# Four conv inputs per layer transposed by VectorE and DRAM scratch instead of TensorE

## The reference, cut to what matters

```python
CONV_WIDTH = 4

def causal_depthwise_conv(x, w, b):
    y = lax.conv_general_dilated(
        x, w[:, None, :], window_strides=(1,), padding=[(CONV_WIDTH - 1, 0)],
        dimension_numbers=('NWC', 'WIO', 'NWC'), feature_group_count=x.shape[-1])
    return y + b

    (aq, ak, av, ag, su, sv, sg, mq, mk, mv, mo, mg, mi, mf) = split_columns(x @ w_in)
...
    qk = jax.nn.silu(causal_depthwise_conv(jnp.concatenate([mq, mk], axis=-1), conv_w, conv_b))
    mq, mk = jnp.split(qk, 2, axis=-1)
...
    h = mlstm_chunkwise(heads(mq), heads(mk) * (MLSTM_HEAD_DIM ** -0.5), heads(mv), ig, lf)
```

## Time and profile before

| what | us |
|---|---|
| median of three runs | 1271.83 (1271.44 to 1271.86) |
| span of the profiled execution, first to last instruction | 1269.9 |
| its own time | not given apart from the three runs; 1.9 lies between its span and their median |
| TensorE busy | 1257.0 (99% of the span) |
| VectorE busy | 893.0 (70%) |
| ScalarE busy | 705.4 (56%) |
| GpSimd busy | 244.0 (19%) |
| DMA, mean | 209 GB/s |

### The profile page before, as it was taken

How to read it: one execution, slowest core, us unless ns; L and a number is a source line. 1 busy time by engine, 2 the same in 40 slices (tenths; PEclk the granted TensorE clock), 3 DMA queues, 4 the chain that set the end, 5 groups by cost and what they waited for, 6 DMA issues and landing times.

```text
span 1269.9 us, 16388 instructions
## 1 busy us (share of the span) xinstructions
PE 1257.0 (99%) x6342; PEld 1040.2 (82%) x6342; DVE 893.0 (70%) x1229; ACT 705.4 (56%) x989; POOL 244.0 (19%) x268
## 2 busy tenths in 40 slices
PE   9999999999999999999999999999999999999996
PEld 8888888878888888888888788888888888888885
DVE  5686876876667655865785779768665776567656
ACT  5477476575555544444563775666755555345441
POOL 0321522522220000400003223334131200004000
PEclk9999999999999999999999999999999999999998
DMA  9968768765665555465657587678546556565562
GB/s 336 310 209 261 236 189 277 260 192 164 204 195 174 184 186 185 152 230 190 207 186 238 183 282 245 193 258 282 184 149 215 183 157 209 165 197 198 186 212 86
DMA packets 129277, 264.97 MB, mean 209 GB/s; under 512 B 8824, under 2 KB 8976, under 8 KB 128688
## 3 DMA queue, kind: packets, MB, share of 16 engines
q1 hardware_dynamic: 123712, 247.23, 60.6%
q0 software_dynamic: 3680, 13.28, 3.0%
q10 hardware_dynamic: 1808, 3.42, 0.7%
HBM read 258.61 MB, written 5.28 MB: 208 GB/s over the span
## 4 chain that ended last, share of the span: by engine, by line
PE 86%; ACT 4%; DVE 4%; POOL 3%; issue 2%; DVEq 0%; POOLq 0%; ACTq 0%
PE ps L373 79%; ACT arena L810 2%; DVE w_lo L1060 2%; ACT w_hi L736 2%; PE ps L444 1%; PE ps L671 1%; PE ps L391 1%; PE ps L639 1%; POOL arena L1684 1%; PE ps L533 0%; POOL arena L1680 0%; PE ps L518 0%; ACT arena L807 0%; PE ps L355 0%; DVE arena L1133 0%
## 5 line engine op out<-in xcount | busy, mean ns | idle before, releaser
L1060 DVE TENSOR_TENSOR w_lo<-w_raw,w_hi 128x1024 fp32r<-128x1024 f32 x408 | 527.1, 1305 | 326.4 <-ACT w_hi L736 324.5
L736 ACT ACTIVATE w_hi<-w_raw 128x1024 fp32r<-128x1024 f32 x408 | 427.3, 1058 | 388.9 <-PE ps L373 339.3
L373 PE MATMUL ps<-w_hi,xT_hi 128*128 128x512 f32 x1616 | 636.2, 394 | 0.7 <-DVE w_lo L1060 0.7
L373 PE MATMUL ps<-w_hi,xT_lo 128*128 128x512 f32 x1616 | 629.6, 390 | 0.0
L373 PE MATMUL ps<-w_lo,xT_hi 128*128 128x512 f32 x1616 | 629.0, 389 | 0.0
L373 PEld LDWEIGHTS ps<-w_hi,xT_hi 128*128 128x128 f32 x1616 | 303.4, 188 | 64.3 <-issue 1.3
L373 PEld LDWEIGHTS ps<-w_hi,xT_lo 128*128 128x128 f32 x1616 | 303.3, 188 | 64.0
L373 PEld LDWEIGHTS ps<-w_lo,xT_hi 128*128 128x128 f32 x1616 | 303.6, 188 | 61.4
L292 POOL TENSOR_TENSOR carried<-ident 1x1 f32<-1x1 f32 x30 | 19.6, 652 | 454.8 <-DVE arena L1416 178.7
L1217 DVE CUSTOM_DVE_ANT_0 mix<-xres,mix 128x1024 f32<-128x1024 f32 x64 | 89.0, 1390 | 1.1
L807 ACT ACTIVATE arena<-arena 32x256 f32<-32x256 f32 x128 | 53.2, 416 | 15.6 <-DVE arena L1137 14.0
(11 more groups left out here) (244 smaller groups left out, 825.3 us busy)
## 6 DMA issues: line engine op xcount, KB each, us to landing
w_raw<-w_in_dram SPq DMA_DIRECT2D x367, 512.0 KB, 4.5
w_raw<-w_out_dram SPq DMA_DIRECT2D x64, 512.0 KB, 4.8
mix<-gate_w_dram SPq DMA_DIRECT2D x32, 512.0 KB, 5.6
xres<-x_dram ACTq DMA_DIRECT2D x4, 512.0 KB, 8.4
v_dram<-arena POOLq DMA_DIRECT2D x4, 512.0 KB, 6.3
z<-v_dram POOLq DMA_DIRECT2D x8, 256.0 KB, 5.6
z<-ln_g_dram POOLq DMA_DIRECT2D x2, 1024.0 KB, 7.7
store<-ln_b_dram POOLq DMA_DIRECT2D x2, 1024.0 KB, 7.9
```

Source lines behind the costliest of these rows:

```text
L373: mm = pe.matmul(ps[2 * s + t][:], a[:, order[c] * KC + k, t * P:(t + 1) * P], b[:, k], start=(c + k + i == 0), stop=(c == CH - 1 and k == ...
L736: A(hi_of(n, c), w_raw[:, c % RING], ACT.Copy).then_inc(w_hi_done, 1)
L1060: TTn(lo_of(n, c), w_raw[:, c % RING], hi_of(n, c).bitcast(F32), ALU.subtract).then_inc(w_lo_done, 1)
```

## The change

TensorE's `conv_transposes` is gone. For each conv input i, VectorE transposes the 32 x 32 blocks of `z` into `conv_zT` (one instruction, 128 x 1024), where every row of 32 positions has 4 words in front. SP puts that to a DRAM scratch (`put`, one DMA of 576 KB in rows of 576 bytes) and fetches it back re-partitioned (`fetch`, four DMAs of 144 KB into 32 partitions each), into `conv_T`, with channels on the partitions. VectorE sets the three older positions in front of each row of 32 (a small memset and a copy), and the convolution's taps are read from there. The put stands in SP's queue behind the last load of block n, the fetch behind the second load of block n + 1. On ScalarE and VectorE the first four splits of block n + 1 move: they now stand between and behind the convolution halves of input i. The last four splits of block n stand behind the transpose on VectorE.

```diff
+QUARTER = P // 4
+HALO = 4
...
+        conv_zT = arena[:, 4096:5248].rearrange("p (f b x) -> p f b x", f=4, x=HALO + QUARTER)
+        conv_T = arena[:, 5248:6400].rearrange("p (b m x) -> p b m x", b=SEQ // QUARTER, x=HALO + QUARTER)
...
+        conv_dram = nc.dram_tensor("conv_dram", (DEPTH, 4, 4, TT, 4, QUARTER, 4 * (HALO + QUARTER)), F32, kind="Internal").ap()
...
+                def put(i):
+
+                    sp.wait_ge(conv_turned, l * 4 + i + 1)
+                    dst = conv_dram[l, i].rearrange("f t u j x -> (u j) (f t) x")
+                    src = conv_zT.rearrange("p f (t m) x -> p (f t) (m x)", t=TT)
+                    sp.dma_start(dst, src).then_inc(conv_put, 16)
+
+                def fetch(i):
+
+                    sp.wait_ge(conv_put, (l * 4 + i + 1) * 16)
+                    src = conv_dram[l, i].rearrange("f t u j x -> f j (t u) x")
+                    dst = conv_T.rearrange("p b m x -> p b (m x)")
+                    for f in range(4):
+                        sp.dma_start(dst[f * QUARTER:(f + 1) * QUARTER], src[f]).then_inc(conv_moved, 16)
...
+                        if c == 1 and N_CONV + 2 <= n <= N_CONV + 5:
+                            fetch(n - N_CONV - 2)
+                        if c == CH - 1 and N_CONV + 1 <= n <= N_CONV + 4:
+                            put(n - N_CONV - 1)
...
-                    chunks(N_CONV + i, Q_CONV + i, i % 2, 0, 2)
-                    conv_transposes(i - 1)
-                    chunks(N_CONV + i, Q_CONV + i, i % 2, 2, 6)
+                    chunks(N_CONV + i, Q_CONV + i, i % 2, 0, 6)
...
-                chunks(N_MV, Q_MV, 0, 0, 2)
-                conv_transposes(3)
-                chunks(N_MV, Q_MV, 0, 2, CH)
+                chunks(N_MV, Q_MV, 0, 0, CH)
...
                 split(N_CONV, 6, 8)
+                split(N_CONV + 1, 0, 4)
                 for i in range(4):
                     n = N_CONV + 1 + i
-                    split(n, 0, 4)
                     take(n, i % 2, z[:, i % 2, 0, :])
-                    split(n, 4, 6)
-                    act.wait_ge(conv_ps, l * 4 + i + 1)
+                    split(n, 4, 8)
+                    act.wait_ge(conv_moved, (l * 4 + i + 1) * 4 * 16)
...
                     for hf in range(2):
-                        split(n, 6 + hf, 7 + hf)
+                        split(n + 1, 2 * hf, 2 * hf + 2)
                         act.wait_ge(conv_done, l * 8 + 2 * i + hf + 1)
...
                 split(N_CONV, 7, 8)
+                split(N_CONV + 1, 0, 4)
                 for i in range(4):
                     n = N_CONV + 1 + i
-                    split(n, 0, 2)
+                    take(n, i % 2, z[:, i % 2, 1, :])
+                    dve.wait_ge(z_act, taken_act(l, Q_CONV + i))
+                    dve.wait_ge(z_dve, taken_dve(l, Q_CONV + i))
+                    V.transpose(conv_zT.rearrange("p f b x -> p b f x")[:, :, :, HALO:],
+                                z[:, i % 2].rearrange("p t c -> p (t c)")).then_inc(conv_turned, 1)
+                    split(n, 4, 6)
...
-                    split(n, 2, 4)
-                    take(n, i % 2, z[:, i % 2, 1, :])
+                    split(n, 6, 8)
+                    dve.wait_ge(conv_moved, (l * 4 + i + 1) * 4 * 16)
+                    V.memset(conv_T[:, 0, :, 1:HALO], 0.0)
+                    own(V.tensor_copy(conv_T[:, 1:, :, 1:HALO], conv_T[:, :-1, :, QUARTER + 1:]))
                     for hf in range(2):
-                        split(n, 4 + 2 * hf, 6 + 2 * hf)
                         dve.wait_ge(conv_bias, l * 8 + 2 * i + hf + 1)
...
-                                y = conv_y[:, hf, t, back:SEQ]
-                                f = STT(y, ps[4 + hf][:, t * SEQ:(t + 1) * SEQ - back], cw[:, m, j:j + 1], y,
-                                        ALU.mult, ALU.add)
+                                y = conv_y[:, hf, t, :].rearrange("p (b s) -> p b s", s=QUARTER)
+                                f = STT(y, conv_T[:, :, 2 * hf + t, HALO - back:HALO - back + QUARTER], cw[:, m, j:j + 1],
+                                        y, ALU.mult, ALU.add)
...
+                        split(n + 1, 2 * hf, 2 * hf + 2)
```

More of the change, by code:

```diff
@@ L236, in hybrid_layers @@
         sgu_ps, sgu_done = sem("sgu_ps"), sem("sgu_done")
-        conv_ps, conv_bias, conv_done, conv_silu = (
-            sem("conv_ps"), sem("conv_bias"), sem("conv_done"), sem("conv_silu"))
+        conv_turned, conv_put, conv_moved, conv_bias, conv_done, conv_silu = (
+            sem("conv_turned"), sem("conv_put"), sem("conv_moved"), sem("conv_bias"), sem("conv_done"), sem("conv_silu"))
         ag_silu, mg_silu, mo_sigmoid = sem("ag_silu"), sem("mg_silu"), sem("mo_sigmoid")
@@ L626, in _ @@
                 chunks(N_SV, Q_SV, 1, 3, CH)
-                def conv_transposes(i):
-                    pe.wait_ge(z_act, taken_act(l, Q_CONV + i))
-                    pe.wait_ge(z_dve, taken_dve(l, Q_CONV + i))
-                    if i == 0:
-                        pe.wait_ge(decay_dve, l + 1)
-                    else:
-                        pe.wait_ge(conv_done, l * 8 + 2 * i)
-                    for m in range(4):
-                        for t in range(TT):
-                            at = ((m % 2) * TT + t) * P
-                            tr = pe.transpose(ps[4 + m // 2][:, at:at + P],
-                                              z[:, i % 2, t, m * P:(m + 1) * P], ident[:])
-                    tr.then_inc(conv_ps, 1)
                 chunks(N_CONV, Q_CONV, 0, 0, CH)
                 for i in range(1, 4):
-                    chunks(N_CONV + i, Q_CONV + i, i % 2, 0, 2)
-                    conv_transposes(i - 1)
-                    chunks(N_CONV + i, Q_CONV + i, i % 2, 2, 6)
+                    chunks(N_CONV + i, Q_CONV + i, i % 2, 0, 6)
                     if i == 1:
@@ L960, in _ @@
                             m = 4 * i + 2 * hf + t
-                            y = A(conv_y[:, hf, t, :], ps[4 + hf][:, t * SEQ:(t + 1) * SEQ], ACT.Identity,
+                            y = A(conv_y[:, hf, t, :].rearrange("p (b s) -> p b s", s=QUARTER),
+                                  conv_T[:, :, 2 * hf + t, HALO:], ACT.Identity,
                                   bias=cb[:, m:m + 1], scale=cw[:, m, 3:4])
@@ L1402, in _ @@
                                 m = 4 * i + 2 * hf + t
-                                y = conv_y[:, hf, t, back:SEQ]
-                                f = STT(y, ps[4 + hf][:, t * SEQ:(t + 1) * SEQ - back], cw[:, m, j:j + 1], y,
-                                        ALU.mult, ALU.add)
+                                y = conv_y[:, hf, t, :].rearrange("p (b s) -> p b s", s=QUARTER)
+                                f = STT(y, conv_T[:, :, 2 * hf + t, HALO - back:HALO - back + QUARTER], cw[:, m, j:j + 1],
+                                        y, ALU.mult, ALU.add)
                             own(f) if j else f.then_inc(conv_done, 1)
+                        split(n + 1, 2 * hf, 2 * hf + 2)
                 n = N_MV + 1
-                split(n, 0, 4)
+                dve.wait_ge(conv_done, (l + 1) * 8)
                 dve.wait_ge(mix_att, l + 1)
```

## The result

| | before | after |
|---|---|---|
| median of the runs, us | 1271.8 (1271.4 to 1271.9) | 1285.1 (1285.1 to 1285.7) |
| ratio, 95% interval | | 1.0107 (1.0093 to 1.0121) |
| span of the profiled execution, us | 1269.9 | 1283.9 |

The forecast was 1265.0 us and the range ended at 1277.0: wrong in sign, and outside the range. What happened is the rival "the loop is longer than the block".

The account below looks back on a forecast made before the run. TensorE, busy 99% of the span, was taken as the bound. From 1271.8 us, 7.0 us of removed transposes gave 1264.8, with the added round trip hidden; forecast 1265.0 us, range 1264.0 to 1277.

Parts of the forecast that it names:

- the loop is longer than the block: Rival, chance 0.19: each transpose waits for the previous input's convolution, TensorE stops at first scores; 1274.8 or 1279.6 us.
- What bounds the kernel, and the 7.0 us removed: TensorE, busy 99%, bounds; removing eight groups of conv transposes at 0.87 us each saves 7.0 us.
- VectorE's added work is hidden as load: On VectorE, 1.3 us more per input, in a window with 7 us free, costs nothing as load.
- The loop, R + 12.85: VectorE's path per input, transpose to next transpose: R + 12.85 us against 21.8 for a block on TensorE.
- R: Time from the end of VectorE's transpose to the last of the four fetches landed.
- the prediction's limit for R: At the scores: the last SiLU is on time if R is at most 9.65 us.
- the prediction's law: Beyond the limit, each us of R costs 8 us in all: time = 1264.8 + 8(R - 9.65).
- R = 8.9: Put 3.7, fetch 5.0 and two hand-overs 0.2 us, leaving 3 us spare at the scores.
- near the price by bytes: Put taken at 3.7 us, from 3.2, 4.7 or 7.7 at 28, 52 or 98 ns per 576-byte row.
- SP's queue: nothing: On SP's queue, chunk 2's load goes out up to 2 us late behind the fetch, yet lands in time: no cost.
- half the rate: Rival, chance 0.10: fetches into a quarter of the partitions take 3.6 us data phase for 1.8; R 10.7, 1273.2 us.
- some 2: Input 3, R near 9: next block's first split finishes some 2 us before TensorE starts block 20.

Follow-up runs that it names:

- e1: Changed kernel without the put and the four fetches, taps reading what VectorE transposed in place: 1264.2 us, ratio 0.9943.
- e2: Changed kernel with the four fetches straight behind the put on SP's queue, no weight load between them: 1266.9 us, ratio 0.9966.
- e3: Changed kernel with one fetch over 128 partitions instead of four over 32, same 576-byte rows and place in the queue: 1269.6 us, ratio 0.9987.
- e9: Changed kernel with four fetches in the old place, each over 128 partitions and two of the eight 576-byte rows: 1271.1 us, ratio 0.9996.
- e4: As e3, but each partition's 4608 bytes lie in one run of the scratch: 1268.0 us, ratio 0.9969.
- e5: Changed kernel with the fetch straight behind the put and as one DMA over 128 partitions: 1264.5 us, ratio 0.9942.
- e6: Changed kernel with the four fetches in the order of quarters 0, 2, 1, 3: 1284.5 us, ratio 1.0098.
- e10: Changed kernel with the four fetches behind the first weight load of the next block, not the second: 1269.8 us, ratio 0.9988.
- e11: Changed kernel with each of VectorE's transposes done twice, one behind the other: 1291.3 us, ratio 1.0150.
- e12: Changed kernel with the next input's copy and transpose one split earlier on VectorE and ScalarE, SP's order unchanged: 1290.5 us, ratio 1.0147.

## Why the prediction was wrong, point by point

- **What bounds the kernel, and the 7.0 us removed**: right. e1 gives 1264.2 for 1264.8.
- **VectorE's added work is hidden as load**: right. The transpose took 1246 ns (1.24 taken), six taps 2.71 (2.6), and GpSimd's product, now at 399.28, met no tap.
- **The loop, R + 12.85**: right in form, 0.2 short, nearly all of it in the bias of half 0 (1.2 us to the first tap, not 1.03). From the last transpose to the end of the last SiLU it is R + 9.5 and to the scores R + 9.65, not R + 9.2 (that this is also the prediction's limit for R is chance). Put into the prediction's law, R as measured gives 1264.8 + 94.8 - 8 x 9.65 = 1282.4; the loops' 1.5 and 2 x 0.4 at the scores make 1284.7, against 1285.1. So the miss is R, and the rest of the sum held.
- **R = 8.9: the step that failed.** The put was taken at 3.7, "near the price by bytes", and took 3.7 and 3.5 only for the first input of a layer, 4.8 to 6.6 later, 4.9 in the mean. The fetch was taken at 5.0 and took 5.8 to 7.8, 6.9 in the mean. R was 11.85: 3 us more, eight times, of which the spare up to 9.65 took 0.75 each. The price of a row was argued over at length (28, 52 or 98 ns), and there the choice was right: 29 ns for the puts' packets and, in e2, e3 and e9, the fetches'. It was not what decided; e4 shows that rows of eight times the size change next to nothing. With the fetch straight behind the put (e2) R is 9.2 in the mean, close to the 8.9.
- **"SP's queue: nothing"** is where the missed size lies. The step asked only what the fetch delays, and answered that rightly (weights were not late in the change). It did not ask what the loads ahead of the fetch do to the fetch, nor what the loads ahead of the put do to the put. By e2, taking the two away from before the fetch is worth 18.2 us. The 4.3 us of a load was used as if it held the contention, but those loads went out one at a time, 33 in 93 us; here a put, two loads, four fetches and a third load go out in 6 us (377.28 to 382.86).
- **The rival "half the rate"** priced the fetch at 6.8 us (5.0 and 1.8 more). In the change it took 6.9 in the mean; what made its R of 10.7 too low is the put, 4.9 and not 3.7. Its 1.8 us are near what e9 takes off a fetch, 1.6, so the transfer into 32 partitions is a cause in its own right, and beside the weight loads this agrees with the Trainium skill (SBUF — State Buffer, Door 1: The DMA port swizzle). With no load ahead of the fetch it hardly shows: e2's fetches go into 32 partitions too and take 4.8 us in the mean, 0.4 over e5's single wide one, and alternating the quarters (e6) gives nothing. So the rival had the size right for the change, in part by luck, since it named a rate that halves everywhere. The two causes do not add: e9 takes 14.0 us off, e2 18.2, and both together (e5) 20.6, which is the floor; either one removed alone brings most of the gain.
- **The slower rival**, "the loop is longer than the block", held in mechanism and place: TensorE waits for `w_lo` behind `conv_moved`, at the first chunk of the next block each time, the last of them just before the scores. It decides from 10.1 and not 10.5. Its two prices, R = 10.9 and 11.5, were both under the mean of 11.85. A chance of 0.19 was too small: of three prices for each transfer the middle ones already made the change slower, and no row showed a transfer close behind two loads, which the choice near the cheap price took for granted. A small slip lies beside it: by the prediction's own terms the first split of block 20 is ready 4.3 us before TensorE needs it at R = 9, not "some 2"; with R as it was, that split came late each time.
- **What was not in the sum**: TensorE's clock fell behind three of its waits. It cost those chunks some 1.7 us each and the end of a layer 0.2 to 0.3 us at the scores, since the rest was waiting time anyway.

**What stays open.** Why a transfer into 32 partitions suffers so much more from weight loads beside it than one into 128: the packets of both last longer, but that does not say where inside the DMA engines or the memory the time goes, and it is not shown that these packets account for all of the 1.6 us. That the loads before the fetch act through bytes still in flight rests on the landing times, the late first packets and e10; no run changed the loads' size. That the loads ahead of the put slow the put rests on e11 alone; e2's puts, with no load behind them, still took 4.4. e12's R of up to 16.5 in layer 2 is not followed up.

## What to carry to other kernels

A step moved through DRAM is a chain of its own: draw the loop (who waits for the put, the fetch, and whose next step starts it), compare its length with the period of the bounding engine, and take the break-even round trip before pricing it. Price the transfers with the queue as it will be, not by the mean share: what is still under way when a transfer that is waited for goes out can cost it more than its own bytes or pieces. If the loop is near the limit, put the fetch straight behind its put, or one load apart with the put moved earlier, and spread it over all partitions; here each of these gave back 14 to 21 of the 21 us.

## What the runs showed that was not expected

- Four DMAs of 144 KB into 32 partitions each, behind two weight loads that were still under way, took 5.8 to 7.8 us (mean 6.9); with no load since the put 4.5 to 5.2 (mean 4.8); the same bytes as four DMAs over 128 partitions behind the same loads 4.5 to 6.0 (mean 5.3).
- Rows of 576 bytes and of 4608 bytes moved 576 KB in nearly the same time (mean fetch 5.1 and 4.9 us, e3 and e4).
- Behind three waits of TensorE (2.4, 2.6, 2.7 us) that broke full work at the upper clock level came a stretch at the lower one: seven or more matmuls of 128 x 512 started 0.43 us apart instead of 0.227, 4.46 us for a chunk of 2.77. Behind three others (2.0, 2.3, 2.3 us) it did not. The length of the wait alone does not decide: in e6 the clock fell behind waits of 2.2 and 3.2 us and not behind one of 2.4.
